# Two decoder blocks on one core: the head of the kernel loads x also in channel order and splits it without transposes

## The chip, the core and the metric

The kernel runs on one core of a Trainium2 chip. The metric is device time in microseconds (us), median of several executions. Engines: TensorE (matmul, PE in the profile), ScalarE (ACT), VectorE (DVE), GpSimd (POOL), SyncE (SP, which issues most DMAs).

## The reference

The input x has 256 tokens and 2048 channels, float32. Two blocks follow each other: a retention layer (8 heads) and a pooling layer, then a gated-delta and convolution layer with gates and a last gated projection. What the change touches is only the first step of the first layer:

```
h = rms_norm(x, g_norm)      # y = x * rsqrt(mean(x*x) + 1e-6) * g
p = h @ w_in                 # 2048 x 12288, columns of q, k, v, z
q, k, v, z = split(p)        # then rope, chunked retention, norm, gate, @ w_out
```

The kernel multiplies x by the channel weights g ahead of the product and applies the row factor rsqrt(...) to the product's results.

## The kernel before

All weights are streamed: 900 chunks of 512 KB, in the order of their use, each two blocks of 128 input channels by 512 output columns. SyncE loads a chunk into one of four slots (`raw`). To keep float32 accuracy, both operands of each product are split in two parts of reduced width: ScalarE copies a chunk to `whi` (`split_hi`, L537), VectorE writes the rest, `raw - whi`, to `wlo` (`split_lo`, L911), and TensorE makes three products per pair: high x high, high x low and low x high (`chunk_a`, L1511 to L1513), 12 matmuls of 128x512 per chunk. The other operand is the activation in channel order, `aH` (high) and `aL` (low), 16 tiles of 128 channels by 256 tokens (columns 0 to 15 below).

**The head.** x comes in token order in four pieces into `H` (512 KB each). TensorE turns each piece with eight transposes into PSUM (`spread`, L1536), ScalarE scales it by the channel weights in `cols` and rounds it to `aH` (`t_split_hi`, L547), VectorE writes the rest to `aL` (`t_split_lo`, L922). `norm1(u)` is this for quarter u, four columns. The transposes need the identity matrix in `con`.

**The order.** Every engine has its own program, written out by hand, and works strictly in it; semaphores join them. SyncE issues `con`, then for u = 0 to 3 a piece of x and chunk u (`cols` behind the first piece), then chunk after chunk, each as soon as its slot was split (`lo_done`); a DMA that waits holds those behind it. ScalarE and VectorE: `norm1(0)`, chunk 0, `norm1(1)`, chunks 1 to 3; then the loop of the first retention head (`head`, R_PER = 24 chunks): at step j the split of chunk j + 4, and behind it, at j = 1 and 3, `norm1(2)` and `norm1(3)`; at j = 4 ScalarE squares `H` for the row factors. The split of chunk j + 4 waits for its landing (`raw_in`) and for the multiplied chunk j. TensorE: transposes of quarters 0 and 1, then chunk j for j = 0, 1, ...; ahead of chunks 2 and 4 the transposes of quarters 2 and 3, ahead of chunks 0, 2, 4, 6 a wait for the four columns of the quarter (`t_lo`). GpSimd loads `rot` (256 KB) and `dmask` (1536 KB) once ScalarE has split four chunks (`hi_done` = 4).

Of the kernel before, what the change touches and what calls it, by code (L numbers as in the profile page):

```python
# [16 lines left out]
F32 = mybir.dt.float32  # L17
# [54 lines left out]
CHUNKS = PG_AT + O_PER * O_N  # L72
LN_AT = 14


# [18 lines left out]
def build(nc, dram):  # L94
    with ExitStack() as outer:
# [31 lines left out]
        with ExitStack() as s:  # L127
            XS = sb(s, "XS", [P, NT, DM])
        with ExitStack() as s:
            oH = sb(s, "oH", [P, 32, SEQ], F32R)  # L130
# [118 lines left out]

        con_in, rot_in = sem("con_in"), sem("rot_in")  # L250
        x_in = [sem(f"x_in{n}") for n in range(4)]
# [72 lines left out]
        def _(sp):  # L324
            sp.dma_start(con[:], dram["con"]).then_inc(con_in, 16)

            x = dram["x"].rearrange("(t p) n -> p t n", p=P)

            def chunk(q, s):

                sp.wait_ge(lo_done, q * RING + (s + 1))
                sp.dma_start(raw[:, s].rearrange("p k n -> p (k n)"), dram["stream"][q * RING + s]).then_inc(raw_in[s], 16)

            for u in range(4):
                sp.dma_start(H[:, :, u * NB:(u + 1) * NB], x[:, :, u * NB:(u + 1) * NB]).then_inc(x_in[u], 16)
                if u == 0:
                    sp.dma_start(cols[:], dram["cols"]).then_inc(con_in, 16)
                chunk(0, u)
            with sp.Fori(1, (D_AT + 2 * RING) // RING) as i:
# [190 lines left out]
        def _(act):  # L530
# [37 lines left out]
            nc.scalar.preload_act_table(ACT.Silu)  # L568
            act.wait_ge(con_in, 32)

            def norm1(u):
                t_split_hi(T_N1 + u, aH, 4 * u, lambda c: C_RN + 4 * u + c, 6 - 2 * (u % 2))

            norm1(0)
            split_hi(0, 0)
            norm1(1)
# [7 lines left out]
            def head(i, first):  # L584
                q = i * (R_PER // RING) + R_AT // RING
                for j in range(R_PER):
                    split_hi(q, j + RING)
                    if first and j in (1, 3):
                        norm1((j + 3) // 2)
                    if first and j == 4:  # L590
                        for b in range(4):
                            squares(M_N1, b, quarter(H, b), XS[:, :, b * NB:(b + 1) * NB])
                    if not first and j == 1:
                        head_tail(i - 1)
                    if j == 11:
# [310 lines left out]
        def _(dve):  # L906
# [26 lines left out]
            dve.sem_inc(h_out, 2)  # L933
            dve.wait_ge(con_in, 32)

            def norm1(u):
                t_split_lo(T_N1 + u, aH, aL, 4 * u, lambda c: C_RN + 4 * u + c, 6 - 2 * (u % 2))

            norm1(0)
            split_lo(0, 0)  # L940
            norm1(1)
# [20 lines left out]
            def head(i, first):  # L962
                q = i * (R_PER // RING) + R_AT // RING
                for j in range(R_PER):
                    split_lo(q, j + RING)
                    if first and j in (1, 3):
                        norm1((j + 3) // 2)
                    if first and j == 5:
# [531 lines left out]
        def _(pe):  # L1500
            mm = nc.tensor.matmul

            def chunk_a(q, j, kt, hi, lo, bank, last):

                s = j % RING

                pe.wait_ge(lo_done, q * RING + (RING + j + 1))
                for k in range(KPC):
                    for t in range(NT):
                        out, tok = PS[:, bank + t], slice(t * P, (t + 1) * P)  # L1510
# [40 lines left out]
            pe.sem_inc(multiplied, RING)  # L1551
            pe.wait_ge(con_in, 32)
            spread(T_N1, 0, H, x_in[0], 16)
            spread(T_N1, 1, H, x_in[1], 16)

# [5 lines left out]
            def head(i, first):  # L1561
                q = i * (R_PER // RING) + R_AT // RING
                for j in range(R_PER):
                    if first and j in (0, 2, 4, 6):
                        if j in (2, 4):
                            spread(T_N1, j // 2 + 1, H, x_in[j // 2 + 1], 16)
                        pe.wait_ge(t_lo, (T_N1 + j // 2 + 1) * QT)
                    chunk_a(q, j, (j % K16) * KPC, aH, aL, 2 * (j // K16), j % K16 == K16 - 1)
                    if not first and j == 1:
                        head_tail(i - 1)  # L1570
                    if j == 11:

                        pe.wait_ge(rope_done, i * 2 + 2)
                        if first:
                            pe.wait_ge(t_lo, T_R * QT)
                        else:
                            pe.wait_ge(t_lo, i * QT + T_R * QT)
# [437 lines left out]
def arrays_of(inputs):  # L2015
    a = {k: np.asarray(v) for k, v in inputs.items()}

    def by_partition(v):
# [3 lines left out]
    arrays = {  # L2022
        "x": a["x"][0],
        "stream": stream(a),
        "cols": np.concatenate([by_partition(a[k]) for k in (
# [32 lines left out]
```

## Time and profile before

| | us |
|---|---|
| median of 3 runs (lowest, highest) | 2748.70 (2748.51, 2749.75) |
| the profiled execution's own time | 2749.76 |
| its span, first to last instruction | 2748.1 |
| TensorE busy | 2690.1 |
| VectorE busy | 1700.1 |
| ScalarE busy | 1252.8 |
| DMA, GB/s over the span | 180 |

The busy times overlap. A long busy time of an engine says that it is in demand; whether it sets the time is read from the chain that ended last and from what ends the idle stretches. The timeline shows instructions by start and duration; a matmul's duration overlaps the next one's, so distances between starts tell the rate.

### The profile page before, as it was taken

How to read it: one execution, taken by the hardware profiler on the slowest of the kernel's cores; microseconds unless marked ns; L12 is line 12 of the kernel's file. 1: busy time of each engine (PE TensorE's matmuls, PEld its weight loads, DVE VectorE, ACT ScalarE, POOL GpSimd, SP SyncE). 2: the span in 40 equal slices, each digit the busy share in tenths (PEclk: the TensorE clock that was granted, in tenths of full speed). 3: DMA queues.
4: the chain of work that ended last, by engine and by line, in shares of the span. 5: the costliest groups of instructions: out<-in, count | busy, mean ns of one | idle time of the engine just before them, and what ended most of it. 6: DMA issues, size and time to landing. Idle time of an engine off the chain costs nothing.

```text
span 2748.1 us, 40906 instructions
## 1 busy us (share of the span) xinstructions
PE 2690.1 (98%) x14658; PEld 2341.3 (85%) x14658; DVE 1700.1 (62%) x2216; ACT 1252.8 (46%) x1513; POOL 166.2 (6%) x338
## 2 busy tenths in 40 slices
PE   8999999999999999999989999999999999999997
PEld 7888888888888888888888989898998999878886
DVE  5555555555455555554566566464889898866564
ACT  5444444444444444444455545353444444364453
POOL 0000000000000000000004040313000000000000
PEclk9999999999999999999999999999999999999999
DMA  7555555555555555555645453544555555556654
GB/s 253 177 183 177 180 177 177 181 179 190 191 189 192 191 191 188 190 201 193 195 135 169 149 173 118 171 142 155 171 190 194 183 194 183 173 179 193 225 172 143
DMA packets 150275, 495.28 MB, mean 180 GB/s; under 512 B 28528, under 2 KB 29264, under 8 KB 149648
## 3 DMA queue, kind: packets, MB, share of 16 engines
q1 hardware_dynamic: 147664, 482.77, 53.7%
q0 software_dynamic: 2496, 10.87, 1.2%
q8 instruction: 84, 1.38, 0.2%
q14 instruction: 31, 0.25, 0.0%
HBM read 490.42 MB, written 3.16 MB: 180 GB/s over the span
## 4 chain that ended last, share of the span: by engine, by line
PE 89%; POOL 3%; DVE 2%; DMA 2%; issue 1%; ACT 1%; SPq 1%; DVEq 0%; ACTq 0%; POOLq 0%
PE PS L1511 22%; PE PS L1513 22%; PE PS L1512 22%; PE PS L1525 5%; PE PS L1527 5%; PE PS L1528 5%; PE PS L1687 2%; POOL xt L477 2%; POOL xi L481 1%; PE PS L1536 1%; PE PS L1694 0%; DVE wlo L911 0%; ACT whi L537 0%; DMA iT<-diag_in 0%; PE PS L1706 0%
## 5 line engine op out<-in xcount | busy, mean ns | idle before, releaser
L911 DVE TENSOR_TENSOR wlo<-raw,whi 128x1024 fp32r<-128x1024 f32 x900 | 1099.5, 1225 | 987.3 <-ACT whi L537 982.5
L537 ACT CAST whi<-raw 128x1024 fp32r<-128x1024 f32 x900 | 943.3, 1051 | 1359.4 <-PE PS L1513 1024.1
L1511 PE MATMUL PS<-whi,aH 128*128 128x512 f32 x1792 | 702.6, 392 | 2.3 <-DVE wlo L911 1.7
L1512 PE MATMUL PS<-wlo,aH 128*128 128x512 f32 x1792 | 698.1, 390 | 0.0
L1513 PE MATMUL PS<-whi,aL 128*128 128x512 f32 x1792 | 698.1, 390 | 0.0
L1525 PE MATMUL PS<-aH,whi 128*128 128x256 f32 x1536 | 442.9, 288 | 1.5 <-DVEq L1309 1.4
L1528 PE MATMUL PS<-aH,wlo 128*128 128x256 f32 x1536 | 437.5, 285 | 2.5 <-issue 2.5
L1527 PE MATMUL PS<-aL,whi 128*128 128x256 f32 x1536 | 437.6, 285 | 0.0
L1511 PEld LDWEIGHTS PS<-whi,aH 128*128 128x128 f32 x1792 | 336.9, 188 | 72.6 <-DVE wlo L911 2.9
L1513 PEld LDWEIGHTS PS<-whi,aL 128*128 128x128 f32 x1792 | 336.8, 188 | 70.4
L1512 PEld LDWEIGHTS PS<-wlo,aH 128*128 128x128 f32 x1792 | 337.1, 188 | 68.2
L1525 PEld LDWEIGHTS PS<-aH,whi 128*128 128x128 f32 x1536 | 297.9, 194 | 3.0 <-DVEq L1309 1.8
L1528 PEld LDWEIGHTS PS<-aH,wlo 128*128 128x128 f32 x1536 | 297.6, 194 | 2.9 <-issue 2.9
L1527 PEld LDWEIGHTS PS<-aL,whi 128*128 128x128 f32 x1536 | 297.9, 194 | 0.2
L1511 PE MATMUL PS<-whi,oH 128*128 128x512 f32 x512 | 199.6, 390 | 0.0
L1513 PE MATMUL PS<-whi,oL 128*128 128x512 f32 x512 | 199.2, 389 | 0.0
L1512 PE MATMUL PS<-wlo,oH 128*128 128x512 f32 x512 | 199.2, 389 | 0.0
L1322 DVE SCALAR_TENSOR_TENSOR yl<-up,wl,yl 128x256 f32<-128x256 f32 x464 | 193.2, 478 | 0.0
L1512 PEld LDWEIGHTS PS<-wlo,oH 128*128 128x128 f32 x512 | 96.1, 188 | 19.9
L1513 PEld LDWEIGHTS PS<-whi,oL 128*128 128x128 f32 x512 | 96.1, 188 | 19.9
L1511 PEld LDWEIGHTS PS<-whi,oH 128*128 128x128 f32 x512 | 96.1, 188 | 19.7
L1511 PE MATMUL PS<-whi,oaH 128*128 128x512 f32 x256 | 99.7, 389 | 0.0
(292 smaller groups left out, 2236.2 us busy)
## 6 DMA issues: line engine op xcount, KB each, us to landing
raw<-in_stream SPq DMA_DIRECT2D x900, 512.0 KB, 3.3
H<-in_x SPq DMA_DIRECT2D x4, 512.0 KB, 7.8
pB<-in_pool_b POOLq DMA_DIRECT2D x4, 512.0 KB, 3.8
dT<-cum_rows SPq DMA_DIRECT2D x8, 256.0 KB, 4.1
iT<-diag_in SPq DMA_DIRECT2D x16, 128.0 KB, 3.4
bg<-in_b_gate POOLq DMA_DIRECT2D x8, 256.0 KB, 4.0
out<-eb SPq DMA_DIRECT2D x4, 512.0 KB, 2.9
dmask<-in_dmask POOLq DMA_DIRECT2D x1, 1536.0 KB, 10.0
```

Source lines behind the costliest of these rows:

```text
L477: nc.gpsimd.tensor_tensor(term, xi[:, 0:rows, n:n + 1].to_broadcast([P, rows, width]), x[:, n:n + 1, n + 1:].to_broadcast([P, rows, width] ...
L481: ins = nc.gpsimd.tensor_tensor(xi[:, 0:rows, n + 1:], xi[:, 0:rows, n + 1:], term, ALU.add)
L537: nc.scalar.copy(whi[:, s], raw[:, s]).then_inc(hi_done, 1)
L911: nc.vector.tensor_tensor(wlo[:, s], raw[:, s], whi[:, s].bitcast(F32), ALU.subtract).then_inc(lo_done, 1)
L1322: nc.vector.scalar_tensor_tensor(out=to, in0=up[:, c, k:k + SEQ], scalar=w, in1=yl[:, c], op0=ALU.mult, op1=ALU.add).then_inc(long_tap[c], 1)
L1511: mm(out, hi[:, kt + k, tok], whi[:, s, k], start=kt + k == 0, stop=False)
L1512: mm(out, hi[:, kt + k, tok], wlo[:, s, k], start=False, stop=False)
L1513: ins = mm(out, lo[:, kt + k, tok], whi[:, s, k], start=False, stop=last and k == KPC - 1)
L1525: mm(half(bank, c), whi[:, s, k, w], aH[:, kt + k], start=kt + k == 0 and c % 2 == 0, stop=False, skip_group_check=True)
L1527: mm(half(bank, c), whi[:, s, k, w], aL[:, kt + k], start=False, stop=False, skip_group_check=True)
L1528: ins = mm(half(bank, c), wlo[:, s, k, w], aH[:, kt + k], start=False, stop=end, skip_group_check=True)
L1687: ins = mm(PS[rows, bank + n, h * P + at:h * P + at + width], lhsT(t, h), rhs(t, h), start=h == 0, stop=True, skip_group_check=True)
```

## The change

`x` is also given in channel order (`xT`, 16 columns of 128 channels by 256 tokens), and a tile for it is added beside `XS`. It is loaded in four pieces of 2, 4, 4 and 6 columns, interleaved with chunks 0 to 3. Chunk 0 comes in two halves with semaphores of their own. `con` and the four pieces of `H` are issued behind chunk 3. ScalarE and VectorE make `aH` and `aL` straight from `xT`; `norm1(2)` and `norm1(3)` stand one step earlier. TensorE's four groups of transposes in the head are gone, and it waits for two more columns per chunk.

```diff
+X_CUT = (0, 2, 6, 10, 16)
...
+            xT = sb(s, "xT", [P, 16, SEQ])
...
@@ sync
-            sp.dma_start(con[:], dram["con"]).then_inc(con_in, 16)
...
+            def piece(u):
+                lo, hi = X_CUT[u], X_CUT[u + 1]
+                sp.dma_start(xT[:, lo:hi], dram["xT"][:, lo:hi]).then_inc(x_in[u], 16)
+
+            sp.dma_start(cols[:], dram["cols"]).then_inc(cols_in, 16)
+            piece(0)
+            sp.dma_start(raw[:, 0, 0], dram["stream"][0][:, 0:NB]).then_inc(first_in, 16)
+            sp.dma_start(raw[:, 0, 1], dram["stream"][0][:, NB:]).then_inc(raw_in[0], 16)
+            piece(1)
+            chunk(0, 1)
+            piece(2)
+            chunk(0, 2)
+            piece(3)
+            chunk(0, 3)
+            sp.dma_start(con[:], dram["con"]).then_inc(con_in, 16)
             for u in range(4):
-                sp.dma_start(H[:, :, u * NB:(u + 1) * NB], x[:, :, u * NB:(u + 1) * NB]).then_inc(x_in[u], 16)
-                if u == 0:
-                    sp.dma_start(cols[:], dram["cols"]).then_inc(con_in, 16)
-                chunk(0, u)
+                sp.dma_start(H[:, :, u * NB:(u + 1) * NB], x[:, :, u * NB:(u + 1) * NB]).then_inc(h_in, 16)
@@ scalar
             def norm1(u):
-                t_split_hi(T_N1 + u, aH, 4 * u, lambda c: C_RN + 4 * u + c, 6 - 2 * (u % 2))
+                act.wait_ge(x_in[u], 16)
+                for k in range(X_CUT[u], X_CUT[u + 1]):
+                    nc.scalar.activation(aH[:, k], xT[:, k], ACT.Copy, scale=cols[:, C_RN + k:C_RN + k + 1]).then_inc(t_hi, 1)
 
             norm1(0)
-            split_hi(0, 0)
+            act.wait_ge(first_in, 16)
+            nc.scalar.copy(whi[:, 0, 0], raw[:, 0, 0]).then_inc(first_hi, 1)
+            act.wait_ge(raw_in[0], 16)
+            nc.scalar.copy(whi[:, 0, 1], raw[:, 0, 1]).then_inc(hi_done, 1)
             norm1(1)
...
                     split_hi(q, j + RING)
-                    if first and j in (1, 3):
-                        norm1((j + 3) // 2)
+                    if first and j in (0, 2):
+                        norm1(j // 2 + 2)
                     if first and j == 4:
+                        act.wait_ge(h_in, 64)
@@ vector: norm1, the two halves of chunk 0 and the steps j in (0, 2) in the same manner
@@ tensor
+                if first:
+                    pe.wait_ge(first_lo, 1)
+                else:
+                    pe.wait_ge(lo_done, q * RING + (RING + j + 1))
                 for k in range(KPC):
+                    if first and k:
+                        pe.wait_ge(lo_done, RING + 1)
...
-            spread(T_N1, 0, H, x_in[0], 16)
-            spread(T_N1, 1, H, x_in[1], 16)
+            pe.sem_inc(t_ps, 8)
...
-                    if first and j in (0, 2, 4, 6):
-                        if j in (2, 4):
-                            spread(T_N1, j // 2 + 1, H, x_in[j // 2 + 1], 16)
-                        pe.wait_ge(t_lo, (T_N1 + j // 2 + 1) * QT)
-                    chunk_a(q, j, (j % K16) * KPC, aH, aL, 2 * (j // K16), j % K16 == K16 - 1)
+                    if first and j < K16:
+                        pe.wait_ge(t_lo, KPC * (j + 1))
+                    chunk_a(q, j, (j % K16) * KPC, aH, aL, 2 * (j // K16), j % K16 == K16 - 1, first and j == 0)
...
                         if first:
+                            pe.wait_ge(con_in, 16)
```

## Rows read from the trace of the kernel before

**Rows 1.** The page, parts 1 and 4: busy time of the engines; chain that ended last.
```profile
PE 2690.1 (98%) x14658; PEld 2341.3 (85%) x14658; DVE 1700.1 (62%) x2216; ACT 1252.8 (46%) x1513; POOL 166.2 (6%) x338
...
PE 89%; POOL 3%; DVE 2%; DMA 2%; issue 1%; ACT 1%; SPq 1%; DVEq 0%; ACTq 0%; POOLq 0%
```
**Rows 2.** Timeline of SyncE's queue (start, duration of the issue, both us).
```profile
1.78 0.47 SPq L337 DMA_DIRECT2D cols<-in_cols  x1
```
**Rows 3.** DMA issues of the first 40 us: KB each, us to landing.
```profile
dmask<-in_dmask POOLq DMA_DIRECT2D x1, 1536.0 KB, 10.0
...
rot<-in_rot POOLq DMA_DIRECT2D x1, 256.0 KB, 5.5
...
con<-in_con SPq DMA_DIRECT2D x1, 256.0 KB, 2.8
...
cols<-in_cols SPq DMA_DIRECT2D x1, 84.5 KB, 4.6
```
**Rows 4.** Timeline of ScalarE, first 75 us (start, duration, idle before and releaser).
```profile
16.32 1.05 ACT L537 CAST whi<-raw 128x1024 fp32r<-128x1024 f32 x1 [1.58 <-DMA raw<-in_stream]
17.58 1.05 ACT L537 CAST whi<-raw 128x1024 fp32r<-128x1024 f32 x1 [0.21 <-DMA raw<-in_stream]
...
19.90 1.56 ACT L547 ACTIVATE aH<-PS,cols 128x256 fp32r<-128x256 f32 x4
...
30.36 0.63 ACT L556 ACTIVATE XS<-H 128x512 f32<-128x512 f32 x1
```
**Rows 5.** Timeline of VectorE, first 32 us.
```profile
17.40 3.85 DVE L911 TENSOR_TENSOR wlo<-raw,whi 128x1024 fp32r<-128x1024 f32 x3 [1.39 <-ACT whi L537]
21.17 1.65 DVE L922 SCALAR_TENSOR_TENSOR aL<-PS,cols,aH 128x256 fp32r<-128x256 f32 x4
```
**Rows 6.** Timeline of TensorE (matmul engine), first 27 us.
```profile
9.84 1.97 PE L1536 MATMUL PS<-con,H 128*128 128x128 f32 x8 [1.47 <-DMA H<-in_x]
11.59 0.76 PE L1511 MATMUL PS<-whi,aH 128*128 128x512 f32 x1
...
14.29 0.63 PE L1511 MATMUL PS<-whi,aH 128*128 128x512 f32 x1
14.71 0.47 PE L1512 MATMUL PS<-wlo,aH 128*128 128x512 f32 x1
15.02 0.39 PE L1513 MATMUL PS<-whi,aL 128*128 128x512 f32 x1
...
22.33 0.39 PE L1511 MATMUL PS<-whi,aH 128*128 128x512 f32 x1
...
25.06 1.03 PE L1536 MATMUL PS<-con,H 128*128 128x128 f32 x8
25.85 0.48 PE L1511 MATMUL PS<-whi,aH 128*128 128x512 f32 x1
```
**Rows 7.** Windows: busy us of each engine, granted clock, DMA share, GB/s moved.
```profile
0.00:5.40 5.40, 0.00 (x0) 0.00 (x0) 0.00 (x0) 1.28 (x1) 0.35 (x6) 1.00 0.67 161
0.00:8.50 8.50, 1.97 (x8) 1.57 (x8) 0.00 (x0) 2.16 (x4) 0.35 (x6) 1.00 0.75 228
0.00:14.40 14.40, 6.53 (x23) 5.40 (x24) 5.35 (x10) 7.17 (x12) 0.35 (x6) 1.00 0.87 298
0.00:15.10 15.10, 7.22 (x25) 5.96 (x26) 6.05 (x11) 7.50 (x12) 0.35 (x6) 1.00 0.88 302
...
7.00:18.00 11.00, 9.53 (x36) 7.73 (x35) 7.57 (x12) 7.69 (x13) 0.00 (x0) 1.00 1.00 388
18.75:28.75 10.00, 10.00 (x54) 8.49 (x53) 6.55 (x9) 6.04 (x11) 0.55 (x2) 1.00 0.92 362
```
**Rows 8.** An idle stretch of TensorE at 1388: windows, then its timeline.
```profile
1391.00:1396.00 5.00, 0.00 (x0) 0.00 (x0) 2.74 (x5) 1.85 (x5) 4.26 (x9) 0.50 0.16 36
1396.00:1400.00 4.00, 3.69 (x17) 3.29 (x17) 2.71 (x8) 2.62 (x7) 2.22 (x4) 0.50 0.72 176
...
1396.18 3.68 PE L1536 MATMUL PS<-con,XS 128*128 128x128 f32 x16 [8.23 <-DVE XS L1117]
```

More of the change, by code:

```diff
@@ L246, in build @@
         block = outer.enter_context(nc.Block())
-        con_in, rot_in = sem("con_in"), sem("rot_in")
+        con_in, cols_in, rot_in, h_in, first_in, first_hi, first_lo = (
+            sem(n) for n in "con_in cols_in rot_in h_in first_in first_hi first_lo".split())
         x_in = [sem(f"x_in{n}") for n in range(4)]
@@ L568, in _ @@
             nc.scalar.preload_act_table(ACT.Silu)
-            act.wait_ge(con_in, 32)
+            act.wait_ge(cols_in, 16)
             def norm1(u):
-                t_split_hi(T_N1 + u, aH, 4 * u, lambda c: C_RN + 4 * u + c, 6 - 2 * (u % 2))
+                act.wait_ge(x_in[u], 16)
+                for k in range(X_CUT[u], X_CUT[u + 1]):
+                    nc.scalar.activation(aH[:, k], xT[:, k], ACT.Copy, scale=cols[:, C_RN + k:C_RN + k + 1]).then_inc(t_hi, 1)
             norm1(0)
-            split_hi(0, 0)
+            act.wait_ge(first_in, 16)
+            nc.scalar.copy(whi[:, 0, 0], raw[:, 0, 0]).then_inc(first_hi, 1)
+            act.wait_ge(raw_in[0], 16)
+            nc.scalar.copy(whi[:, 0, 1], raw[:, 0, 1]).then_inc(hi_done, 1)
             norm1(1)
@@ L933, in _ @@
             dve.sem_inc(h_out, 2)
-            dve.wait_ge(con_in, 32)
             def norm1(u):
-                t_split_lo(T_N1 + u, aH, aL, 4 * u, lambda c: C_RN + 4 * u + c, 6 - 2 * (u % 2))
+                for k in range(X_CUT[u], X_CUT[u + 1]):
+                    dve.wait_ge(t_hi, k + 1)
+                    nc.vector.scalar_tensor_tensor(out=aL[:, k], in0=xT[:, k], scalar=cols[:, C_RN + k:C_RN + k + 1],
+                                                   in1=aH[:, k].bitcast(F32), op0=ALU.mult,
+                                                   op1=ALU.subtract).then_inc(t_lo, 1)
             norm1(0)
-            split_lo(0, 0)
+            dve.wait_ge(first_hi, 1)
+            nc.vector.tensor_tensor(wlo[:, 0, 0], raw[:, 0, 0], whi[:, 0, 0].bitcast(F32), ALU.subtract).then_inc(first_lo, 1)
+            dve.wait_ge(hi_done, 1)
+            nc.vector.tensor_tensor(wlo[:, 0, 1], raw[:, 0, 1], whi[:, 0, 1].bitcast(F32), ALU.subtract).then_inc(lo_done, 1)
             norm1(1)
@@ L965, in head @@
                     split_lo(q, j + RING)
-                    if first and j in (1, 3):
-                        norm1((j + 3) // 2)
+                    if first and j in (0, 2):
+                        norm1(j // 2 + 2)
                     if first and j == 5:
@@ L1501, in _, with chunk_a @@
             mm = nc.tensor.matmul
-            def chunk_a(q, j, kt, hi, lo, bank, last):
+            def chunk_a(q, j, kt, hi, lo, bank, last, first=False):
                 s = j % RING
-                pe.wait_ge(lo_done, q * RING + (RING + j + 1))
+                if first:
+                    pe.wait_ge(first_lo, 1)
+                else:
+                    pe.wait_ge(lo_done, q * RING + (RING + j + 1))
                 for k in range(KPC):
+                    if first and k:
+                        pe.wait_ge(lo_done, RING + 1)
                     for t in range(NT):
@@ L1551, in _ @@
             pe.sem_inc(multiplied, RING)
-            pe.wait_ge(con_in, 32)
-            spread(T_N1, 0, H, x_in[0], 16)
-            spread(T_N1, 1, H, x_in[1], 16)
+            pe.sem_inc(t_ps, 8)
             def head_tail(i):
@@ L2023, in arrays_of @@
         "x": a["x"][0],
+        "xT": a["x"][0].T.reshape(16, P, SEQ).transpose(1, 0, 2),
         "stream": stream(a),
```

## Prediction

> **What bounds the kernel now.** I read the shares of the span and the chain of waits first [rows 1]: TensorE is busy 2690.1 of 2748.1 us and holds 89% of the chain, so time is won or lost only where TensorE idles or does extra work. The change touches only the first 40 us or so, so I read that stretch engine by engine. On TensorE [rows 6]: a second group of eight transposes starts at 9.84, the first weight matmul at 11.59, and from there to the end of the head there is no gap. Up to 14.71 the matmuls start every 0.42 us (from 14.29 to 14.71), later every 0.23 (chunk 3 runs from 22.33 to 25.06: 12 matmuls, 2.73 us). By that pace these are TensorE's lower and upper clock level, 1.2 and 2.4 GHz, though the granted clock in the windows reads 1.00 from the start [rows 7]. Two more groups of transposes stand between chunks; the one at 25.06 pushes chunk 4 to 25.85, 0.8 us. Then the DMA side [rows 2, 3, 7]: from 7 to 18 us the engines are full (share 1.00, 388 GB/s). So in the head the order in which SyncE issues transfers decides when each one lands.
>
> **A rule for landings, out of the trace.** SyncE's issues go through one hardware queue. Before, `cols` (84.5 KB) is issued third, behind `con` and an x piece, and takes 4.6 us to land where `con`, three times its size and first in the queue, takes 2.8 [rows 2, 3]: transfers land in issue order. I count bytes: the x piece that releases TensorE at 9.84 [rows 6] ends 1.92 MB of issued transfers, and 8.5 us x 228 GB/s = 1.94 MB had moved by 8.5 [rows 7]: it is seen 1.3 us after its bytes. Chunk 3, whose landing starts ScalarE at 16.32 [rows 4], ends 4.54 MB; 15.1 x 302 = 4.56 MB: 1.2 us. So: landing = time at which the bytes up to and with it have moved, plus 1.2 us.
>
> **The change part by part.**
>
> *Start.* `cols`, x columns 0 and 1 (256 KB) and half a chunk (256 KB) make 0.61 MB. 5.4 x 161 = 0.87 MB had moved by 5.4 [rows 7], about 0.28 MB/us in that stretch, so 0.61 MB at about 4.4; landing by 5.3 to 5.6. Then a half-chunk copy (the nearest row, a 128x512 pass on ScalarE, is 0.6 [rows 4]) and a half-chunk subtract (half of 3.85/3, 0.65 [rows 5]): first matmul at about 6.7 instead of 11.59. At the lower level chunk 0 lasts 12 x 0.42 = 5.1, to 11.8. Chunk 1 ends 1.92 MB: landed 9.8, but ScalarE first does four columns of 0.39 [rows 4], so its copy ends at about 11.1, the subtract at 12.3. Chunk 2 ends 2.97 MB, moved at about 11.1 (between 1.94 at 8.5 and 14.4 x 298 = 4.29 at 14.4 [rows 7]), landed 12.3, split by 14.7. TensorE: chunk 1 from 12.4, chunk 2 from 15.1 to 17.9. Before, chunk 3 starts at 22.33 [rows 6], so here the new kernel is 4.4 us ahead.
>
> *Chunk 3.* In the new order chunk 3 (columns 6 and 7) waits for eight split columns, `t_lo` >= 8. Columns 6 to 9 are made by `norm1(2)`, which on both ScalarE and VectorE stands **behind the split of chunk 4** (the loop does `split(j + RING)` and then `norm1` at j = 0). And chunk 4 is issued behind everything in the new list: `cols` 0.087, x in channel order 2.097, chunks 0 to 3 2.097, `con` 0.262, then H 2.097 MB, chunk 4 0.524: it ends 7.16 MB, where before it ended 5.07. All that is gained ahead of chunk 3 is lost in this wait, so the estimates of the start don't reach the end.
>
> *When chunk 4 lands.* Chunk 3 ends 4.28 MB, moved at 14.4 [rows 7]: landed 15.6, copied 16.7. That copy (`hi_done` = 4) releases GpSimd's `rot` and `dmask` (1.84 MB), whose landings took 5.5 and 10.0 us before [rows 3]; they share the DMA engines with what is left of the 2.88 MB of `con`, H and chunk 4. Lower end: GpSimd's transfers take nothing: 2.88/0.388 = 7.4, moved at 21.8, landed 23.0. Upper end: they all go first: (2.88 + 1.84)/0.37 = 12.8, landed 28.4. Between: from 18.75 to 28.75 before, when `dmask` was under way, 3.62 MB moved [rows 7], of which at most 1.84 GpSimd's, so both sides had about half. With half each from about 17.5: 0.388 x 3.1 = 1.20 by then, 1.68 left at 0.18 to 0.19 MB/us takes 9.1, moved 26.6, landed 27.8. If GpSimd's bytes start 1.5 us after the issue, the remainder is 1.10 MB and it lands at 26.1. I take 27.2.
> By the Trainium skill ("DMA: Bandwidth & Descriptors", Queues, rings and completion order) each DMA engine takes turns between its queues packet by packet. By that rule the pieces of H, in runs of 2 KB, would get less than half against the long rows of `dmask`, and chunk 4 would land nearer 28.4, a time 1.2 us above mine. No row here separates packets from bytes. The same page (Bandwidth) puts what one core reads from HBM at about 358 GB/s; this trace shows 388 over 11 us, and the measurement decides.
>
> *From there to TensorE.* Copy of chunk 4 1.05 [rows 4], its subtract 1.3, columns 6 and 7 at 0.41 each [rows 5]; ScalarE makes the columns beside the subtract. With handovers 3.2: chunk 3 starts at 30.4, after 12.5 us of idle TensorE. Queued behind chunk 4's split are the splits of 5 and 6 and `norm1(3)`; chunk 5 would land at about 29 and is split by 32.6, columns 10 and 11 by 34.6, all ahead of their use.
>
> *Clock.* The trace has one such gap: 8.23 us idle before 1396.18 [rows 8]. In it the granted clock goes to 0.50, and it is 0.50 up to 1400. After the start at 9.84 the lower level also stays until about 14.7: the next start is at 15.02 [rows 6]. So 4 to 5 us of chunk 3 run at half speed: 2.0 to 2.4 us lost; I take 2.2. A bound from below is nothing, if the clock held.
>
> *Sum.* Chunk 4 then starts at 30.4 + 2.7 + 2.2 = 35.3, without the transposes. Before it started at 25.85: 9.4 us later. Behind this point the order is as before: the squares of H begin after the split of chunk 8 (before at 30.36 [rows 4]) and need 4.9 us; chunk 9's split follows at 44.9 and ends at about 46.2, and TensorE wants it at 35.3 + 5 x 2.73 = 48.9. H, `con`, `rot` and `dmask` have landed by then. Nothing catches up, as TensorE is the bound from there, and its later idle stretches hang on work that shifts with it. The edits of semaphores, the moved `con` and the tile for x cost nothing: no wait on them is late. I take 9.3. Profiled execution: 2749.76 + 9.3 = 2759.1. That execution stands 1.06 over the median of the runs, so **2748.7 + 9.3 = 2758.0 us.** With landings from 26.1 to 28.4 and 2.0 to 2.4 for the clock the case itself spans 2756.7 to 2759.4 (2755.8 if the clock held).
>
> **The rivals.**
> 1. *GpSimd's transfers hardly count* (chance 7%). Chunk 4 lands at 23.0 to 24.5; chunk 3 at 26.2 to 27.7, idle enough for the clock to fall; chunk 4 of TensorE at 31.1 and up: +5.3, 2754.0, to 2755.5. For it: hardly a row; `rot` needed 5.5 us for 256 KB, so its bytes start late. Against: `dmask` landed in 10.0 us.
> 2. *Faster* (8%): H doesn't hold chunk 4, that is, later transfers overtake the pieces of H in the queue and chunk 4 lands as before, about 17.6 [rows 4]. Then chunk 3 starts at 20.8, the clock hardly falls, chunk 4 at 23.5 instead of 25.85: -2.3, 2746.4; if it lands before 15, the whole gain, 17.9 against 22.33 and one group of transposes of 0.8, gives -5.2, 2743.5. It decides for faster if chunk 4 lands before about 19.9 (3.2 + 2.73 ahead of 25.85). For it: several transfers are in flight at once. Against: the landing of `cols`, and the byte counts above, which fit issue order at two points.
> 3. *The delay is absorbed* (5%): a later stage is bound by something that does not move, and the time stays within 2 us of 2748.7. Against: TensorE's 89% of the chain; no transfer later is tied to the start.
>
> The forecast has 80%. About 0.2% (5.5 us) is what a measurement of this kernel can tell from no change. Faster: rival 2, 0.08. Within: rival 3 and half of rival 1, 0.09. Slower 0.83. The range reaches down into rival 1, to 2753.5, and up to 2761, for a lower DMA rate while H, with its 2 KB rows, and `dmask` move together (0.33 MB/us would put the landing at 29.9).
>
> **What the new profile would show.** Right: weight matmuls from about 6.7; TensorE idle of about 12 us before chunk 3 near 30, behind VectorE's `aL`, which is behind ScalarE waiting for the DMA of `raw`; clock 0.50 in it; no idle in the next 100 us; DMA share near 1 from 3 to 30 us. Wrong: ScalarE's copy of chunk 4 before 20 us (rival 2), or at 23 (rival 1), or an idle stretch later that shrinks by what the head lost (rival 3).

## Result and the profile after

The changed kernel is slower than before, and slower than predicted. Its median is 2767.39 us (4 runs, 2764.33 to 2768.99) against 2749.22 (4 runs, 2748.51 to 2750.94): ratio 1.0064, 95% interval 1.0049 to 1.0079, or +18 us where +9.3 was forecast. The profiled execution is the shortest of the four, 2764.33 us; its span is 2762.7, 14.6 us over the one before. All places below are counted in this pair of spans.

The page of the kernel after: span, part 1, a queue of part 3, part 4.
```profile
span 2762.7 us, 40849 instructions
PE 2690.4 (97%) x14626; PEld 2339.7 (85%) x14626; DVE 1700.4 (62%) x2217; ACT 1253.3 (45%) x1514; POOL 166.2 (6%) x338
...
q8 instruction: 102, 1.67, 0.2%
...
PE 87%; POOL 4%; DVE 2%; DMA 2%; issue 2%; SPq 1%; ACT 1%; DVEq 0%; ACTq 0%; POOLq 0%
```
TensorE does no more work than before [rows 1], 2690.4 against 2690.1 us, though its 32 transposes of the head are gone: less work, and a longer span. In part 3 one queue of instructions has grown. Its row of the kernel before (packets, MB, share):
```profile
q8 instruction: 84, 1.38, 0.2%
```
**The head.** TensorE's timeline after, cut to the starts of chunks 0, 1 and 2, the last matmul of chunk 2, and chunks 3 and 4:
```profile
7.88 0.76 PE L1540 MATMUL PS<-whi,aH 128*128 128x512 f32 x1 [7.88 <-DVE wlo L962]
...
13.04 0.47 PE L1540 MATMUL PS<-whi,aH 128*128 128x512 f32 x1 [0.16 <-DVE wlo L930]
...
15.86 0.39 PE L1540 MATMUL PS<-whi,aH 128*128 128x512 f32 x1
...
18.36 0.39 PE L1542 MATMUL PS<-whi,aL 128*128 128x512 f32 x1
27.66 0.80 PE L1540 MATMUL PS<-whi,aH 128*128 128x512 f32 x1 [8.92 <-DVE aL L956]
...
32.83 0.40 PE L1540 MATMUL PS<-whi,aH 128*128 128x512 f32 x1
```
It answers to [rows 6]: chunk 0 starts 3.7 us earlier than before, chunk 4 starts 7.0 us later (32.83 against 25.85), with 8.92 us of idleness ahead of chunk 3, ended by VectorE's `aL`. ScalarE's timeline says what that hung on. The copies are those of chunks 3 and 4, and the activation is `norm1(2)`:
```profile
16.00 1.05 ACT L550 CAST whi<-raw 128x1024 fp32r<-128x1024 f32 x1 [2.16 <-DMA raw<-in_stream]
24.51 1.04 ACT L550 CAST whi<-raw 128x1024 fp32r<-128x1024 f32 x1 [7.45 <-DMA raw<-in_stream]
25.46 1.70 ACT L587 ACTIVATE aH<-xT,cols 128x256 fp32r<-128x256 f32 x4
```
Chunk 4 lands at about 24.4, behind H. The windows after show the engines of the DMA full until then, and the granted clock in the idle stretch and after it:
```profile
16.00:25.00 9.00, 2.74 (x13) 1.93 (x11) 1.22 (x1) 1.54 (x2) 1.29 (x2) 0.86 1.05 404
25.00:28.00 3.00, 0.34 (x1) 0.34 (x2) 2.41 (x5) 2.16 (x5) 0.00 (x0) 0.50 0.99 415
28.00:33.00 5.00, 5.00 (x13) 3.90 (x13) 3.24 (x5) 3.74 (x7) 0.00 (x0) 0.53 0.78 291
```
**Beyond the head.** TensorE's transposes are marks that both kernels pass with the same work between them. By line and operand, count: duration min/median/max in ns, first to last start in us. Before:
```profile
L1536 PE MATMUL PS<-con,oR x64: 270/272/273, 90.1 to 584.1; 128*128 128x128 f32 x64
...
L1536 PE MATMUL PS<-con,XS x32: 270/347/476, 1396.2 to 1413.5; 128*128 128x128 f32 x32
...
L1536 PE MATMUL PS<-con,oD x32: 272/272/273, 1582.0 to 1944.1; 128*128 128x128 f32 x32
...
L1536 PE MATMUL PS<-con,yl x32: 270/272/273, 2482.2 to 2551.0; 128*128 128x128 f32 x32
```
and after:
```profile
L1565 PE MATMUL PS<-con,oR x64: 270/272/273, 97.0 to 591.0; 128*128 128x128 f32 x64
...
L1565 PE MATMUL PS<-con,XS x32: 270/347/473, 1403.2 to 1420.8; 128*128 128x128 f32 x32
...
L1565 PE MATMUL PS<-con,oD x32: 272/273/273, 1592.8 to 1955.4; 128*128 128x128 f32 x32
L1565 PE MATMUL PS<-con,yl x32: 270/272/273, 2496.8 to 2565.6; 128*128 128x128 f32 x32
```
The offset is 6.9 us at the first `oR`, and still 7.0 at the first `XS`, 1300 us on. At the last `oD` it is 11.3, at the first `yl` 14.6, and 14.6 at the last `yl`. So the head lost 7.0, the gated-delta stage (first `XS` to last `oD`) 4.3 and the gate stage (to the first `yl`) 3.3, and no line that the change touches runs in those two. This second part, 7.6 of 14.6 us, was nowhere in the prediction.

The waits of TensorE in the delta stage show part of it (total us, times, longest). Before:
```profile
PE PS L1706 <- DVE iT L1161: 7.7, 4, 2.9
```
after:
```profile
PE PS L1732 <- DVE iT L1185: 13.0, 4, 4.4
```
And in the gate stage, within a chunk that is loaded and split, TensorE stops for nothing that the profile shows. Its timeline after:
```profile
2251.86 0.28 PE L1556 MATMUL PS<-aL,whi 128*128 128x256 f32 x1
2253.60 0.39 PE L1557 MATMUL PS<-aH,wlo 128*128 128x256 f32 x1 [1.46 <-issue]
```
The instruction queue in the window from 1955 to 2490, first the kernel before:
```profile
q8 instruction: 14, 0.23, 0.2%
```
then after:
```profile
q8 instruction: 32, 0.52, 0.4%
```
18 of the 18 additional packets lie there (102 - 84). One packet is 1.67 MB / 102 = 16.4 KB. The traces show where they go. The gate stage has a loop of three passes, and the branch at the end of the first two goes back to its start. Those branches, in the queue that takes TensorE's instructions in order (PEldq in the rows; duration min/median/max in ns, first to last start in us; the third one leaves the loop) are, before and after:
```profile
L1855 PEldq COMPARE_BRANCH  x3: 76/218/233, 2119.4 to 2344.8; - x3
...
L1881 PEldq COMPARE_BRANCH  x3: 76/3808/4351, 2130.8 to 2360.0; - x3
```
Before, queue q8 moves nothing from 2119.5 to 2344.5, that is, in the second and third pass. After, each of these two passes (2131 to 2245, 2245.5 to 2360) has
```profile
q8 instruction: 9, 0.15, 0.6%
```
and lasts 114.6 us instead of 112.7: 3.9 us in the two, less 0.6 that the stage takes back behind the loop. So the gate loop's code is loaded again in each pass. The loop of the delta stage is loaded again in both kernels, 9 packets in the second and 9 in the third pass, with branches of 3.3 to 3.5 us in both; before:
```profile
L1823 PEldq COMPARE_BRANCH  x3: 83/3339/3452, 1627.3 to 1875.0; - x3
```
The additional packets gave the theory that the experiments tested, called **placement** below: the change takes 62 instructions out of TensorE's program (32 transposes of two instructions each, less two new waits), so the loops behind lie 62 instructions nearer to its start. If code is fetched in blocks of fixed size, a loop can then touch one block more than the chip keeps, and is fetched again in each pass. Its rival, **phase**: the head's delay moves the later stages against something that does not move. For the head the theory was the prediction's (chunk 4 behind H, `norm1(2)` behind chunk 4).

### The profile page after: what moved, and what is told of

It is laid out like the page before. It is cut to its first block, busy times and chain, and to the rows that moved or that the text cites. A ratio compares the mean times of both kernels' runs of the same rounds, so it can differ in the third digit from the quotient of the medians.

```text
span 2762.7 us, 40849 instructions
## 1 busy us (share of the span) xinstructions
PE 2690.4 (97%) x14626; PEld 2339.7 (85%) x14626; DVE 1700.4 (62%) x2217; ACT 1253.3 (45%) x1514; POOL 166.2 (6%) x338
## 3 DMA queue, kind: packets, MB, share of 16 engines
q8 instruction: 102, 1.67, 0.2%
## 4 chain that ended last, share of the span: by engine, by line
PE 87%; POOL 4%; DVE 2%; DMA 2%; issue 2%; SPq 1%; ACT 1%; DVEq 0%; ACTq 0%; POOLq 0%
PE PS L1540 22%; PE PS L1542 22%; PE PS L1541 22%; PE PS L1554 5%; PE PS L1557 5%; PE PS L1556 5%; POOL xi L494 2%; POOL xt L490 2%; PE PS L1713 2%; PE PS L1565 1%; DMA iT<-diag_in 1%; DVE wlo L930 0%; DMA raw<-in_stream 0%; ACT whi L550 0%; PE PS L1732 0%
```

## The experiments

"Filler" below is an increment of a semaphore that nothing waits for, put into TensorE's program. Each ratio is against the kernel before on the same chip, where its median was 2749 to 2752 us, so the medians of the table can't be divided by its first row. pad62, norm_early, h_late and both_pad62 were timed beside each other, so were before_pad194, before_delay, pad62_late and best, and so were after_again, pad126_late, pad190_late and best2. The stage columns are from the profiled execution; packets are those of q8.

| kernel | median us | ratio (95%) | chunk 4 starts | first `oR` | delta stage | gate stage | packets |
|---|---|---|---|---|---|---|---|
| before | 2749.2 | | 25.85 | 90.1 | 547.9 | 538.1 | 84 |
| after | 2767.39 | 1.0064 (1.0049 to 1.0079) | 32.83 | 97.0 | 552.2 | 541.4 | 102 |
| after_again | 2765.11 | 1.0049 (1.0030 to 1.0068) | 32.37 | 96.8 | 553.1 | 540.2 | 102 |
| pad62 | 2754.04 | 1.0012 (1.0003 to 1.0021) | 32.01 | 96.2 | 544.4 | 537.7 | 84 |
| pad62_late | 2753.45 | 1.0015 (1.0006 to 1.0024) | 32.72 | 96.9 | 548.2 | 537.8 | 84 |
| pad126_late | 2763.31 | 1.0035 (1.0024 to 1.0046) | 32.75 | 96.9 | 548.0 | 538.3 | 84 |
| pad190_late | 2782.37 | 1.0103 (1.0084 to 1.0122) | 32.83 | 97.3 | 555.7 | 538.2 | 85 |
| before_pad194 | 2771.27 | 1.0071 (1.0058 to 1.0084) | 35.29 | 99.8 | 555.9 | 540.4 | 103 |
| before_delay | 2758.97 | 1.0035 (1.0026 to 1.0044) | 35.65 | 99.9 | 551.2 | 538.0 | 84 |
| norm_early | 2762.02 | 1.0047 (1.0030 to 1.0064) | 27.17 | 93.4 | 551.1 | 543.8 | 102 |
| h_late | 2760.19 | 1.0036 (1.0022 to 1.0050) | 23.89 | 91.7 | 556.6 | 539.2 | 102 |
| both_pad62 | 2748.20 | 0.9996 (0.9986 to 1.0006) | 24.52 | 94.6 | 540.9 | 538.0 | 84 |
| best | 2749.72 | 0.9996 (0.9988 to 1.0005) | 21.27 | 90.5 | 547.7 | 537.8 | 84 |
| best2 | 2746.67 | 0.9983 (0.9972 to 0.9994) | 20.77 | 89.4 | 544.7 | 538.3 | 84 |

The branches back to the start of the gate loop take 3.6 to 4.7 us in all five traces with 102 or 103 packets, and 0.22 or 0.23 us in the nine others. Those of the delta loop take 3.3 to 3.9 us in all fourteen.

**after_again** is the kernel after, unedited, beside the others.

> The changed kernel as it is, timed again beside the others of this study. 102 fetches; 1.0055 to 1.0075 of the kernel before (2764 to 2770 us). This is the value that the two runs with more filler are compared with.

Measured: 1.0049, the same packets, the same stages within 1.2 us. The intervals overlap: what the change costs is between 0.3 and 0.8%, 13 to 18 us by the two medians' ratios.

**pad62**: the 62 instructions come back, as fillers at the start of TensorE's program.
```diff
             pe.sem_inc(multiplied, RING)
+            for _ in range(62):
+                pe.sem_inc(sem("pad"), 1)
```


> The changed kernel plus 62 filler instructions (increments of an unused semaphore) at the start of TensorE's program, where TensorE waits 7.9 us for its first data anyway. The change took 62 instructions out of TensorE's program, so this puts every later loop of it back to its old offset. Theory code: the 7.9 us that the changed kernel loses after the head (offset +6.9 us at the end of the head, +11.3 at 1955, +14.6 at 2497) come from instructions being fetched again in TensorE's loops; then the extra loss of 3.3 us in the gate stage (2058 to 2400 us) goes, and perhaps part of the 4.3 in the delta stage: span 2762.7 down to 2755 to 2759, and no instruction fetches between 2130 and 2350 us. Theory time: the later loss follows from the later start of the stages alone (transfers and GpSimd fall into another phase); then the span stays at 2762 to 2767.

Measured: 1.0012, 84 packets, the gate stage back at 537.7, and 62 additional instructions make the kernel about 10 us faster (1.0049 to 1.0012, timed on different chips; norm_early and h_late, timed beside pad62 and without fillers, stand at 1.0047 and 1.0036 though their heads are shorter). The fillers delay the first matmul by 3.0 us (10.84 instead of 7.88), which is lost again in the wait for chunk 3: chunk 4 starts at 32.01. They take much longer than 3.0 us, most of it while TensorE waits for its first data anyway:
```profile
L1582 PEldq EVENT_SEMAPHORE  x62: 51/51/51, 1.1 to 10.4; - x62
```
Its waits in the delta stage and its packets from 1955 to 2490:
```profile
PE PS L1734 <- DVE iT L1185: 5.9, 4, 2.2
...
q8 instruction: 14, 0.23, 0.2%
```
The wait for `iT` has gone from 13.0 to 5.9 us, by instructions of TensorE alone. This doesn't separate the two theories fully, since the head shifted by 0.8 us as well.

**pad62_late**: the same fillers ahead of the transposes of `XS`, at about 1400 us, where TensorE idles 8.2 us anyway [rows 8]; everything up to there is as in after.
```diff
             def norm3(u):
                 spread(T_N3, u, XS, rows_sb, NT * (u + 1))
+            for _ in range(62):
+                pe.sem_inc(sem("pad"), 1)
```


> The changed kernel with the 62 fillers ahead of the layer-2 transposes (TensorE idles 8.2 us there) instead of at the start: only the delta loop, the gate loop and what follows get their old place, the retention and pooling loops keep the new one. Theory code, as far as the delta and gate loops are the ones that matter: the same 84 fetches and the same time as with the fillers at the start, 2752 to 2756. If the earlier loops matter: 2760 and more.

Measured: 1.0015, 84 packets, `oR` at 96.9 and `XS` at 1403.0 as in after, then delta 548.2 and gate 537.8 as before. The phase is that of after within 0.2 us, and the loss of the later stages is gone. That speaks for placement, and the head alone costs what is left: 4 us by the ratio (1.7 to 6.6), 6.9 by the marks.

**before_delay**: the kernel before with a delay of its first transposes by one added wait.
```diff
             pe.wait_ge(con_in, 32)
+            pe.wait_ge(raw_in[3], 16)
             spread(T_N1, 0, H, x_in[0], 16)
```


> The kernel before, with TensorE's first transposes made to wait for chunk 3 (landed at 16.2 us); the number of instructions is the same. The first matmul then comes near 18 to 19 us instead of 11.6, and the head ends some 5 to 7 us later. Theory code: the delay is carried through to the end and nothing is added: 2755 to 2757, 84 fetches. Theory time (a later start alone costs more in the delta and gate stages): 2760 and more.

Measured: +9.8 us at the first `oR` and 1.0035 in all, +9.6 us (7.1 to 12.1). 84 packets, gate 538.0. The delay at the head is more than the 5 to 7 us foreseen. It is carried to the end one for one, and calls up none of the additional packets: phase is refuted for the gate stage. For the delta stage it isn't that clean, as it took 551.2 us here. The windows of that stage (width; busy PE, PEld, DVE, ACT, POOL; granted clock) show what it consists of. before_delay:
```profile
1406.00:1957.00 551.00, 527.98 (x3976) 507.17 (x3977) 325.63 (x532) 267.32 (x362) 134.93 (x279) 0.97 0.47 150
```
before:
```profile
1396.00:1944.00 548.00, 523.41 (x3977) 502.64 (x3978) 325.45 (x533) 267.44 (x362) 135.38 (x279) 0.98 0.47 151
```
after:
```profile
1403.00:1955.00 552.00, 524.44 (x3974) 504.06 (x3975) 325.60 (x533) 267.18 (x362) 135.38 (x279) 0.97 0.46 150
```
and both_pad62:
```profile
1400.00:1941.00 541.00, 517.50 (x3972) 496.48 (x3973) 326.13 (x534) 267.08 (x361) 136.07 (x280) 0.99 0.48 153
```
Width less busy time is idle time: 23.0, 24.6, 27.6 and 23.5 us. Nearly the same matmuls keep TensorE busy for 517.5 to 528.0 us, the more the lower the mean granted clock is (0.99 to 0.97). So the time of this stage has two parts: idle time, which among these four is largest with the placement of after, and the clock, beside which the busy time moved by up to 10 us. Over all fourteen traces the idle time separates the placements: 22.3 to 24.6 us, with 5.3 to 7.7 us of waits for `iT`, in the seven with the placement of before, and 25.2 to 29.1 us, with 10.9 to 14.8 us of waits, in the five with that of after. What decides how often the clock falls here was not tried. A difference of a few us in the delta column can't be read as placement without the wait for `iT` beside it.

**before_pad194**: the reverse. If blocks hold 256 instructions, 194 more have the effect of 62 fewer. The Trainium skill ("Advanced Engine Details and Errata", ISA Cache) states such a block: lines of 16 KB, 256 instructions each, 128 KB of them on TensorE. The 16.4 KB of a packet agree with it. 97 stand at the start, 97 ahead of the transposes of `XS`.
```diff
+            for _ in range(97):
+                pe.sem_inc(sem("pad"), 1)
...
             def norm3(u):
                 spread(T_N3, u, XS, rows_sb, NT * (u + 1))
+            for _ in range(97):
+                pe.sem_inc(sem("pad"), 1)
```


> The kernel before, with 194 filler instructions in TensorE's program, 97 at its start and 97 ahead of the layer-2 transposes, both where TensorE waits anyway (6.4 and 8.2 us; a filler took 54 ns, 97 take 5.2 us). 194 is 256 minus 62: if instructions are loaded in blocks of 256 (the 18 extra fetches of the changed kernel moved 0.29 MB, 16 KB each, and an instruction has 64 bytes), the later loops then lie in their blocks as in the changed kernel. Theory code: about 102 fetches instead of 84, some of them between 2130 and 2350 us, and 7 to 12 us slower than the kernel before, with the head unchanged. Rival (the filler of the changed kernel helped by its delay or by chance, or any filler helps): as the kernel before, within 2 us, or faster.

Measured: 1.0071. The kernel before, with nothing of the change in it, now fetches as after does:
```profile
q8 instruction: 103, 1.69, 0.2%
```
and TensorE's waits in the delta stage are
```profile
PE PS L1710 <- DVE iT L1161: 14.8, 4, 5.2
PE PS L1536 <- issue: 11.0, 1, 11.0
```
with delta 555.9 and gate 540.4, 10.3 us over before for the two. The rest, 9.7 at the head and 2.8 at 1400 us, is the time that the fillers take, which is why the loss is more than the 7 to 12 us foreseen with the head unchanged. The packets of after come from where the loops lie, and they come back with 256 - 62. For the period of 256 the runs show just this, 62 fewer and 194 more giving the same picture.

**pad126_late and pad190_late**: after, with 126 and 190 fillers in the place of 62, that is 64 and 128 instructions behind the placement of before.
```diff
-            for _ in range(62):
+            for _ in range(126):
```


> The changed kernel with 126 fillers (62 + 64) ahead of the layer-2 transposes. By counting instructions from the start of TensorE's program, the gate loop (1582 instructions) then touches 7 blocks of 256 as in the kernel before, not 8, and so does the delta loop (1661). Theory code (what counts is the number of blocks that a loop touches): 84 fetches, the gate stage 538 us long, time as with 62 fillers plus what 64 more fillers cost at that place beyond the idle time (6.8 us against 8.2: nothing), 1.001 to 1.003. Rival (only the very offset of the kernel before is good): 102 fetches, 1.0055 or more.

> The changed kernel with 190 fillers (62 + 128) at the same place; they take 10.3 us where 8.2 are idle, so 2 to 3 us are their own cost, to be seen ahead of the delta stage. By the same count the gate loop touches 7 blocks, the delta loop 8. Theory code with both loops counting by themselves: 84 fetches and a gate stage of 538 us, but a delta stage of about 554 as in the changed kernel instead of 547. If the two go together: delta stage near 547.

Measured: 1.0035 and 1.0103; 84 and 85 packets, gate 538.3 and 538.2, so of four placements, 0, +64, +128 and -62, only the last has the additional packets. The delta stage is at 548.0 and 555.7, with 10.0 and 13.0 us of waits for `iT`. 190 fillers thus lengthen the wait for `iT` without a single additional packet of note: packets and that wait are two effects of placement, not one. The number of blocks was counted wrongly for the delta loop: a pass has 880 matmuls, 880 weight loads and 53 other instructions in the trace, 1813 and not 1661, or 7.1 blocks of 256. So it lies in 8 or 9 blocks wherever it starts, which fits that it is loaded again in each pass at every placement.

The price of the fillers was set too low as well. They were to vanish in the 8.2 us of idleness, or nearly so; in truth `XS` starts 6.9 and 16.7 us late. The wait of pad126_late at 1400 and its fillers show how:
```profile
PE PS L1565 <- issue: 15.1, 1, 15.1
...
L1704 PEldq EVENT_SEMAPHORE  x126: 51/51/51, 1390.6 to 1409.7; - x126
```
126 fillers in 19.1 us are 153 ns each, as were the 62 at the start of pad62 (9.3 us, 152 ns each). They start 4 us ahead of the end of the last matmul, and 62 of them are through at 1399.9, ahead of the data for `XS` at 1403. The expectations had 54 ns, from the 3 us by which the first matmul of pad62 came late; but those 3 us are only what stuck out of the first wait. In pad126_late the matmuls still start every 0.23 us while the first fillers run, and the granted clock is 1.00 up to 1397 and 0.50 from 1399 to 1409.7. The distance between fillers is the same on both sides, 151 ns for most.

**norm_early**: `norm1(2)` stands ahead of the split of chunk 3, `norm1(3)` ahead of that of chunk 4 (ScalarE, and VectorE alike); `H` stays where it is.
```diff
             for j in range(1, RING):
+                if j == 3:
+                    norm1(2)
                 split_hi(0, j)
+            norm1(3)
...
-                    if first and j in (0, 2):
-                        norm1(j // 2 + 2)
```


> The changed kernel with norm1(2) put ahead of the split of chunk 3 and norm1(3) ahead of the split of chunk 4, on ScalarE and VectorE. My theory (chunk 3 is held by the order of the engines, not by its own data): chunk 3 starts near 18.4 instead of 27.7, and the wait moves to chunk 4, which starts near 27 (its landing at 24.5 plus 2.4) against 32.8, at the lower clock for 4 to 5 us: the head ends 3 to 5 us earlier than in the changed kernel. Rival (chunk 3 is bound by transfers): no difference.

Measured: chunk 3 starts at 18.82 (after: 27.66), then TensorE waits 5.45 us for chunk 4 itself, which it multiplies from 27.17. `oR` is 3.6 us earlier than after, as foreseen; ratio 1.0047, 102 packets. Of the 7 us of the head, the order of `norm1(2)` makes about half; the landing of chunk 4 makes the rest.

**h_late**: the pieces of `H` are issued behind chunks 4, 5, 6 and 7; the order of the splits is that of after.
```diff
             for u in range(4):
+                chunk(1, u)
                 sp.dma_start(H[:, :, u * NB:(u + 1) * NB], x[:, :, u * NB:(u + 1) * NB]).then_inc(h_in, 16)
-            with sp.Fori(1, (D_AT + 2 * RING) // RING) as i:
+            with sp.Fori(2, (D_AT + 2 * RING) // RING) as i:
```


> The changed kernel with the four pieces of H issued behind chunks 4, 5, 6 and 7, one each, instead of all ahead of chunk 4; norm1(2) still behind the split of chunk 4. My theory (chunk 4 lands late because 2 MB of H stand ahead of it): chunk 4 lands at about 17.6 instead of 24.5, chunk 3 starts at about 20.8 instead of 27.7, without a loss of the clock, so the head ends about 9 us earlier than in the changed kernel, 2 us ahead of the kernel before: time about 9 us under the changed kernel. Rival (GpSimd's loads or the DMA rate hold chunk 4): less than 3 us.

Measured: ScalarE copies chunk 4 at 17.87, chunk 3 starts at 21.03 and chunk 4 at 23.89, 2.0 us earlier than before, as foreseen. `oR` still comes 1.6 us later than before, 5.3 us earlier than after instead of about 9. What was gained by chunk 4 goes again by chunk 9, for which TensorE waits 2.39 us at 41.0: ScalarE sees chunks 7 and 8 only at 30.15 and 32.78, does the squares of `H` behind them, and the split of chunk 9 is late. The ratio, 1.0036, has the loss by placement still in it (102 packets; delta 556.6).

**both_pad62**: H late, `norm1(2)` ahead of the split of chunk 3 and `norm1(3)` behind that of chunk 4, and 62 fillers at the start.

> H behind chunks 4 to 7, norm1(2) ahead of the split of chunk 3, norm1(3) behind that of chunk 4, and the 62 filler instructions. No idle in the head after the first matmul: chunk 3 at 18.4, chunk 4 at 21.1 to 21.5, against 25.85 before, so the head ends 4 to 5 us ahead of the kernel before. If the filler restores the later stages: 2744 to 2746 us. If the later loss follows from anything else in the change: 2748 to 2753.

Measured: 0.9996 (0.9986 to 1.0006), no difference from before. Foreseen were 2744 to 2746 us with the placement restored. It is restored (gate stage 538.0), but the head isn't ahead: the first `oR` comes 4.5 us later than before, and in the profile only a delta stage of 540.9 us, the shortest and with the highest clock, makes up for it. The fillers delay the first matmul to 10.84 us. With both faults mended and the placement restored, the change brings nothing. The later part of the head has a new limit, in TensorE's timeline:
```profile
41.02 0.80 PE L1545 MATMUL PS<-whi,aH 128*128 128x512 f32 x1 [2.69 <-DVE wlo L933]
```
and in ScalarE's (chunks 7 and 8 by their landing, then the squares until 38.7):
```profile
30.18 1.05 ACT L551 CAST whi<-raw 128x1024 fp32r<-128x1024 f32 x1 [5.38 <-DMA raw<-in_stream]
32.81 1.05 ACT L551 CAST whi<-raw 128x1024 fp32r<-128x1024 f32 x1 [1.58 <-DMA raw<-in_stream]
```
x is now loaded twice, 2.1 MB, some 5 us at the 404 GB/s that the head of after moved while its DMA engines were full (an estimate).

**best and best2** take this up, with H and `norm1` placed as in both_pad62. In both, `dmask` has a semaphore of its own and is issued later, and the squares are one piece a step from j = 4 to 7; the fillers stand ahead of the transposes of `XS`, where 62 of them cost nothing. best holds `dmask` until `hi_done` is 9 and moves the rope to j = 8; best2 holds it until 13 and leaves the rope at 7.
```diff
-            pool.dma_start(dmask[:], dram["dmask"]).then_inc(rot_in, 16)
+            pool.wait_ge(hi_done, 13)
+            pool.dma_start(dmask[:], dram["dmask"]).then_inc(sem("dmask_in"), 16)
...
-                    if first and j == 4:
-                        act.wait_ge(h_in, 64)
-                        for b in range(4):
-                            squares(M_N1, b, quarter(H, b), XS[:, :, b * NB:(b + 1) * NB])
+                    if first and 4 <= j < 8:
+                        if j == 4:
+                            act.wait_ge(h_in, 64)
+                        squares(M_N1, j - 4, quarter(H, j - 4), XS[:, :, (j - 4) * NB:(j - 3) * NB])
```


> Everything together: H behind chunks 4 to 7, norm1(2) ahead of the split of chunk 3, norm1(3) behind that of chunk 4, the load of dmask held until nine chunks are split (its use waits for it by itself), the squares of H one piece per chunk from chunk 8 to 11 (rope one step later), 62 fillers ahead of the layer-2 transposes. In the kernel with the filler at the start the head still lost 10.8 - 7.6 = 3.2 us to the fillers, 2.7 and 2.6 us ahead of chunks 9 and 10 to the squares and to chunks 7 and 8 landing at 30 and 33 us. Expected: first matmul near 7.6, no idle ahead of chunk 10, chunk 9 near 35 against 39.7 before: head 4 to 5 us ahead of the kernel before, 2743 to 2746. Rival (the 2 MB more of x keep the transfers behind TensorE whatever the order): chunk 9 at 38 or later and 2747 or more.

> As the kernel with everything together, but the row factors and rope at their old step (behind the split of chunk 11, ahead of that of chunk 12), and dmask held until 13 chunks are split. In that kernel chunk 12 landed at 39.4 beside dmask, rope ended at 46.3, and chunk 12 started at 47.45 against 48.5 before, chunk 13 at 51.7 against 51.3: the 4.7 us won by chunk 9 were gone. Expected: rope ends near 44, chunk 12 starts at 45 to 45.5, so the head ends 3 us ahead of the kernel before, 0.9985 to 0.999. Rival (the next wait takes it again: the splits of chunks 12 to 14 behind rope): nothing won, 0.9995 to 1.

Measured: best 0.9996, as before, where 2743 to 2746 us were foreseen: TensorE waits 3.2 us for the roped operand. best2 0.9983 (0.9972 to 0.9994), the one version whose interval lies below the kernel before, by some 4.7 us of 2749. Its matmuls run from 7.34 (before 11.59) without a gap to the same wait:
```profile
7.34 0.77 PE L1548 MATMUL PS<-whi,aH 128*128 128x512 f32 x1 [7.34 <-DVE wlo L966]
...
45.18 1.17 PE L1615 MATMUL PS<-con,roped 128*128 128x128 f32 x8 [2.46 <-DVE roped L990]
```
The lead is 5.2 us at the start of chunk 11 (39.83 against 44.98), 2.2 at chunk 12 behind that wait, and 0.7 at chunk 13: chunk 12 starts at the lower clock level, 0.43 us from matmul to matmul, and lasts 4.3 us, against 2.8 before. At the first `oR` it is still 0.7, where 3 were foreseen. The rest of the 3.6 us between the spans is the delta stage (544.7 against 547.9), where the clock scatters; the interval allows a gain from 1.6 to 7.7 us. That the gain comes from the head beyond these 0.7 us is not shown.

## Why the prediction was wrong

Its direction was right and its time too low. By its own steps:

- *Start.* Foreseen: first matmul at 6.7, chunk 1 at 12.4, chunk 2 at 15.1. Measured: 7.88, 13.04, 15.86, each 0.6 to 1.2 late, and of no effect, as it said, since all of it is lost ahead of chunk 3.
- *Chunk 3 behind `norm1(2)` behind chunk 4 behind H.* Right: [rows 4] had the copy of chunk 4 without a wait, and the two rows of after show 7.45 us of waiting and `aH` behind it. norm_early and h_late each undo one link, and chunk 3 starts at 18.8 and 21.0.
- *When chunk 4 lands.* Foreseen 27.2 (bounds 23.0 and 28.4), measured about 24.4: it went as rival 1 had it. The mis-sized part is the start of GpSimd's bytes. I had them share from 17.5, or 1.5 us after the issue. The queues after, from 17.5 to 21 us, from 22 to 24.5 and from 24.5 to 27 (packets, MB):
```profile
q1 hardware_dynamic: 661, 1.37, 106.0%
...
q0 software_dynamic: 104, 0.67, 66.4%
q1 hardware_dynamic: 104, 0.39, 38.9%
...
q0 software_dynamic: 68, 0.84, 79.3%
q1 hardware_dynamic: 68, 0.24, 23.4%
```
  `rot` was issued at 17.70 and `dmask` at 18.44, and up to 21.5 nothing of theirs moved; their first packet starts at 21.8. By then nearly all of the bytes up to chunk 4 had moved: 4.88 MB at 16.0 (305 GB/s), 1.95 more by 21.0, 0.36 more by 22.0, 7.19 in all against the 7.16 of the sum. By the rule for landings that gives 23.2, against 24.4 seen. So the rule is 1.2 us short here, where it fitted at two points before. In the missing stretch SyncE's queue had 0.39 of 1.06 MB; that the last packets of chunk 4 were held up by this is argued, not shown.
  The prediction had both sides get half of the bytes, from a mean over 10 us. The rows show halves of another kind: 104 packets each, then 68 each, with 0.39 MB against 0.67 and 0.24 against 0.84. The prediction also weighed a rule of the Trainium skill ("DMA: Bandwidth & Descriptors", Queues, rings and completion order), turns packet by packet, with a landing at 28.4. The trace agrees with the turns, by these equal numbers of packets, and not with the landing, which was 4 us earlier because GpSimd's packets started so late.
- *From there to TensorE, and the clock.* 3.2 us foreseen from landing to chunk 3, 3.3 measured (24.4 to 27.66). Clock loss 2.2 foreseen; chunk 3 lasts 5.17 us, 2.4 over the 2.73 of [rows 6]. Right.
- *Chunk 4 at 35.3*, measured 32.83: the 2.5 us are the landing's, which came 2.8 earlier than foreseen. Head +9.3 foreseen, +7.0 measured, so the head was forecast too long by 2.3 us, and hid as much of the miss below.
- *"Nothing catches up", the offset is carried to the end, and what else is edited costs nothing.* **This is the step that failed.** The first half holds: 7.0 us after 1300 us, and in before_delay 9.8 at the head and 9.6 in all. The second half doesn't: the removal of 62 instructions (32 transposes of two instructions, less two waits), which the sum counted only as time saved in the head, goes with a loss of 7.6 us in the two profiles, and of about 10 by the runs with and without 62 fillers (1.0049 against 1.0012 and 1.0015). Added to the head's 7.0 the 7.6 make the 14.6 between the two spans. The 18 us between the medians hold 3.6 more that the profiled execution, the shortest of its four, doesn't show.

Shown: the loss comes and goes with instructions that do nothing, in the changed kernel and in the one before. Shown too, for the gate stage: the code of its loop is loaded again in each pass, 9 packets each, its branches back take 3.6 to 4.7 us instead of 0.2, and two passes take 1.9 us longer each. A pass of this loop has 1582 instructions, 6.2 blocks of 256, and so lies in 7 or 8 of them, by its place; that 7 stay and 8 don't is inferred from the count. Still open: by which way placement lengthens the wait for `iT` in the delta stage, whose loop is loaded again at every placement, where the number of packets stays (36 and 35) and which pad190_late lengthens too.

## What to carry to other kernels

When TensorE bounds a long program with large loops, a change in the number of its instructions anywhere ahead of them is a term of the sum: compare the packets of the instruction queue and the durations of the loops' branches of both kernels first, and run the new one once with fillers that restore the old count before any of the difference is put down to the change itself. In a head that is bound by DMA, find what the first wait hangs on in issue order, and write down which split stands behind which landing; loading an operand a second time to save 32 transposes only moves the limit. Read a long difference off common marks (here the transposes), stage by stage, and look at the granted clock of each stage before a few microseconds get a cause.

## What the runs showed of the hardware

- 62 instructions fewer made the kernel about 10 us slower, 62 semaphore increments made good for it; placements 0, +64 and +128 gave 84 or 85 packets, -62 and +194 gave 102 and 103.
- A branch back to the start of a large loop (over 1500 instructions) took TensorE 0.22 or 0.23 us where the loop's code stayed, and 3.3 to 4.7 us where it was loaded again. Where the gate loop's stayed, queue q8 moved no packet in two passes.
- A TensorE semaphore increment took 153 ns on average (126 in pad126_late), the same with the granted clock at 1.00 and, behind its fall, at 0.50. This clock does not slow it.
- GpSimd's transfers moved no byte for 3 us after the issue of `dmask` (18.44 to 21.5), behind a full queue of SyncE. With both at work the two queues had equal numbers of packets (104 and 104, 68 and 68), so the one with the larger packets had more bytes.
- The core moved 404 GB/s over 9 us and 415 over 3. The prediction held 388 against the 358 that the Trainium skill gives for one core; its page "Perfetto Trace Analysis" (Roofline) says that this is the share with both cores of a pair at work and that one alone can pull more, up to about 435. These rows agree.
- The same delta stage had TensorE busy from 517.5 to 528.0 us in different kernels, with a mean granted clock from 0.99 to 0.97.
